# Splitting the end of each sub-layer in a two-layer decoder trunk by quarters of the residual, and moving the x transposes ahead of the last quarter and behind two k steps

## The chip, the cores and the metric

The kernel runs on 1 core of one Trainium2 chip. The time is device microseconds of one execution; before the change the median of 3 runs is 1054.25 us (1053.63 to 1054.94).

## What is computed

One sequence of 256 tokens, width 1024, goes through two layers in float32. Each layer has three sub-layers that write into x, and so six sub-layer ends, the last of which is the end of the kernel:

```python
for l in range(DEPTH):                       # DEPTH = 2
    x = x + 0.5 * swiglu(rms_norm(x, ffn1_norm[l]), ffn1_w_gate[l], ffn1_w_up[l], ffn1_w_down[l])
    h = rms_norm(x, mix_norm[l])
    proj = h @ w_in[l]                       # q, k, v, latents, rope key, two gates
    ...                                      # sliding-window attention and latent attention
    merged = sigmoid(g_a) * (o_a @ w_branch_a[l]) + sigmoid(g_b) * (o_b @ w_branch_b[l])
    x = x + merged @ w_out[l]
    x = x + 0.5 * swiglu(rms_norm(x, ffn2_norm[l]), ffn2_w_gate[l], ffn2_w_up[l], ffn2_w_down[l])
```

with `swiglu(x, g, u, d) = (silu(x @ g) * (x @ u)) @ d`, and an inner width of 2816.

## The kernel before

Every weight and every activation is split into a high part (fp32r) and a low part (the rest), and a product is three matmuls: high by high, high by low, low by high. ScalarE (ACT) writes the high part of a weight block, VectorE (DVE) the low part, and TensorE (PE) multiplies. SyncE loads a block when the slot's last low part has been written.

**FFN.** The inner width is 22 blocks of 128. `gate_up` makes gate and up of a block (8 k steps each, into PSUM banks 2b and 2b + 1, b = block parity), ACT and DVE turn them into aTh and aTl, and `down` adds the block's share of the result to the banks 4 to 7. The result has four quarters q = h * 2 + t, where h is the half of 512 columns and t the half of 128 tokens; each quarter is one bank, and takes 3 matmuls of 512 columns for a block. The loop runs `gate_up(e + 1)`, `down(e)`, and after it comes `down(21)` alone, with `stop=True` (L1450, L1485). Its quarters 0 to 2 each count up `acc_done`, the last one `d_used`.

**The end of a sub-layer.** DVE adds the quarters to x (`residual`, L943 to 955), one instruction each, and counts up `x_done`. PE transposes x to have its columns on the partitions (`columns`, L1329 to 1338): 8 columns chunks c of 128, 2 transposes each, the first four chunks when the quarters 0 and 1 of x are there, the other four when quarter 3 is. Chunk 6 and 7 reuse the banks of chunk 0 and 1, and wait until those were read (`ht_lo`). ACT multiplies a chunk by the norm's gain and writes its high part (`columns_high`, L576), DVE its low part (`columns_low`, L962). ACT squares three of the quarters for the norm (`squares`, L569, in `norm`), DVE the fourth (`last_square`, L880), then DVE adds them (`mean_square`, L887 and L889) and GpSimd (POOL) makes the inverse root (L429). ACT and DVE each work their list strictly as it is written:

```python
                def norm(n):                       # ACT
                    squares(n, 0)
                    columns_high(n)
                    squares(n, 1, (0,))
```

```python
                residual(0)                        # DVE
                columns_low(1)
                last_square(1)
                mean_square(1)
                for k in range(1, GATE1 + 1):
                    split_mix(k)
```

**What follows the end.** After the first FFN of a layer the mixer begins: PE runs the first half of gate block 0 (4 k steps of 6 matmuls of 512 columns, on chunk k), then eight `proj` blocks. Their low parts are what `split_mix(1)`, `split_mix(2)` and so on make (L833); that of gate block 0 was made within the FFN. `block_ready` makes PE wait for a block's low part. After the mixer (its last product is `w_out`, 4 blocks, 6 matmuls per quarter) and after the second FFN of layer 0 an FFN begins: `gate_up_first` takes 8 k steps of 4 matmuls, and then `spread_rs` (L1340), which multiplies the inverse root out over the partitions and waits for POOL's result. The raw sums of the gates don't depend on the root, so that nothing before needs it.

Of the kernel before, what the change touches and what calls it, by code (L numbers as in the profile page):

```python
# [59 lines left out]
X_BANK = (2, 3, 4, 6, 5, 7, 2, 3)  # L60
# [32 lines left out]
def build(nc, x_in, pos_in, cols_in, rows_in, w_ffn, w_proj, w_gate, w_uq, w_ukv, w_branch, w_out,  # L93
          masks_in, freq_in, out):
    with ExitStack() as ctx:
# [194 lines left out]
        def start_cols(i):  # L290

            c = (i % 2) * KC * P + (i // 2) * HALF
            return slice(c, c + HALF)

# [189 lines left out]
        def _(act):  # L484
# [7 lines left out]
            for l in range(DEPTH):  # L492
# [79 lines left out]
                def columns_high(n, part=range(KC)):  # L572
                    act.wait_ge(small_in.sem, small_in.per_layer * (l + 1))
                    for c in part:
                        act.wait_ge(ht_ps.sem, ht_ps.at(l, KC * n + c))
                        act.activation(hTh[:, c, :], ps[:, X_BANK[c], c // 6 * SEQ:(c // 6 + 1) * SEQ], ACT.Copy,  # L576
                                       scale=cols[:, 7 + n * KC + c:8 + n * KC + c]).then_inc(ht_hi.sem, 1)
# [245 lines left out]
        def _(dve):  # L823
# [4 lines left out]
            for l in range(DEPTH):  # L828
# [113 lines left out]
                def residual(n):  # L942

                    for h in range(2):
                        for t in range(TT):
                            q = h * TT + t
                            if q < 3:
                                dve.wait_ge(acc_done.sem, acc_done.at(l, 3 * n + q))
                            elif n == 1:
                                dve.wait_ge(gu_used.sem, gu_used.at(l, FFN2_0 - 1))  # L950
                            else:
                                dve.wait_ge(d_used.sem, d_used.at(l, FB * (n // 2 + 1) - 1))
                            part = x[:, t, h * HALF:(h + 1) * HALF]
                            factor = 0.5 if n == 1 else half_rs[:, t:t + 1]
                            dve.scalar_tensor_tensor(out=part, in0=ps[:, 4 + 2 * t + h, :], scalar=factor, in1=part,  # L955
                                                     op0=ALU.mult, op1=ALU.add).then_inc(x_done.sem, 1)

                def columns_low(n, part=range(KC)):
                    dve.wait_ge(small_in.sem, small_in.per_layer * (l + 1))
                    for c in part:  # L960
                        dve.wait_ge(ht_hi.sem, ht_hi.at(l, KC * n + c))
                        dve.scalar_tensor_tensor(out=hTl[:, c, :], in0=ps[:, X_BANK[c], c // 6 * SEQ:(c // 6 + 1) * SEQ],  # L962
# [72 lines left out]
                residual(0)  # L1035
# [9 lines left out]
                columns_low(1)  # L1045
# [238 lines left out]
                residual(1)  # L1284
                columns_low(2)
# [3 lines left out]
                residual(2)  # L1289
                if l + 1 < DEPTH:  # L1290
                    l += 1
                    columns_low(0)
# [5 lines left out]
        def _(pe):  # L1298
# [17 lines left out]
            for l in range(DEPTH):  # L1316
                def columns_start():
# [3 lines left out]
                    for c in range(KC):  # L1321
                        if c >= 6:
                            pe.wait_ge(ht_lo.sem, ht_lo.at(0, c - 6))
                        for t in range(TT):
                            ins = pe.transpose(ps[:, X_BANK[c], c // 6 * SEQ + t * P:c // 6 * SEQ + (t + 1) * P],  # L1325
                                               x[:, t, c * P:(c + 1) * P], ident[:, :])
                        ins.then_inc(ht_ps.sem, 1)

                def columns(n):  # L1329

                    for h in range(2):
                        pe.wait_ge(x_done.sem, x_done.at(l, 4 * n + (h + 1) * TT - 1 - 2 * TT))
                        for c in range(4 * h, 4 * h + 4):
                            if c >= 6:
                                pe.wait_ge(ht_lo.sem, ht_lo.at(l, KC * n + c - 6))
                            for t in range(TT):
                                ins = pe.transpose(ps[:, X_BANK[c], c // 6 * SEQ + t * P:c // 6 * SEQ + (t + 1) * P],  # L1337
                                                   x[:, t, c * P:(c + 1) * P], ident[:, :])
                            ins.then_inc(ht_ps.sem, 1)
# [34 lines left out]
                def gate_up_first(w):  # L1374
# [4 lines left out]
                    for k in range(KC):  # L1379
                        pe.wait_ge(ht_lo.sem, ht_lo.at(l, 2 * w * KC + k))  # L1380
# [69 lines left out]
                def down(w, i2, e, start=False, stop=False):  # L1450
# [4 lines left out]
                    for h in range(2):  # L1455
                        for t in range(TT):
                            ins = act_by_weight(ps[:, 4 + 2 * t + h, :], aTh[:, b, t * P:(t + 1) * P],
                                                aTl[:, b, t * P:(t + 1) * P], wh_d[b][:, h * HALF:(h + 1) * HALF],
                                                wl_d[b][:, h * HALF:(h + 1) * HALF], start, stop)
                            if stop and h * TT + t < 3:  # L1460
                                ins.then_inc(acc_done.sem, 1)
                    ins.then_inc(d_used.sem, 1)

                def ffn(w):
                    if l + w == 0:
                        columns_start()
                    else:
                        columns(2 * w)
# [12 lines left out]
                    with pe.Fori(first, FB // 2 - 1) as i:  # L1481
# [250 lines left out]
                for j in range(4):  # L1732
# [14 lines left out]
                ffn(1)  # L1747
# [63 lines left out]
```

## Time and profile before

| what | value |
|---|---|
| median of 3 runs | 1054.25 us (1053.63 to 1054.94) |
| span of the profiled execution, first to last instruction | 1051.9 us |
| what lies around the span, by the median | 2.35 us |
| granted TensorE clock over the span | 1.000 |
| busy: TensorE matmul | 1046.4 us |
| busy: TensorE weight load | 899.3 us |
| busy: VectorE | 721.1 us |
| busy: ScalarE | 593.3 us |
| DMA | 187.55 MB, mean 178 GB/s |

The profiled execution has no time of its own beside its span: the three runs shown lie 1.7 to 3.0 us above it. Busy time of TensorE's matmuls is modelled at their ends, which overlap the start of the next one, so that a short wait between two of them may not show as idle; the weight loads (PEld) show it.

### The profile page before, as it was taken

The numbers are of one execution on the slowest core, as the hardware profiler recorded it, in microseconds if no ns is written. First come the engines' busy times: TensorE is split into PE (matmuls) and PEld (weight loads), VectorE is DVE, ScalarE is ACT, GpSimd is POOL, SyncE is SP. The second block draws the span as 40 slices with busy tenths as digits, with TensorE's granted clock in tenths as the row PEclk, the third lists the DMA queues.
The fourth block names the chain that finished last, engine by engine and source line by source line (L and its number), as shares of the span: only waits on it lengthen the run. The fifth ranks groups of instructions, "written<-read, shape, count | busy, mean of one in ns | idle before, by whom it ended". The sixth has DMA issues, their size and how long they took to land.

```text
span 1051.9 us, 15566 instructions
## 1 busy us (share of the span) xinstructions
PE 1046.4 (99%) x5664; PEld 899.3 (85%) x5664; DVE 721.1 (69%) x1132; ACT 593.3 (56%) x931; POOL 66.0 (6%) x69
## 2 busy tenths in 40 slices
PE   9999999999999999999999999999999999999998
PEld 8888888898888888888888888889988888888887
DVE  6766666668786776666686666666697867666664
ACT  6555555467864655555565555555688556555552
POOL 1042000122100000000000000001211000000000
PEclk9999999999999999999999999999999999999999
DMA  7655554455335454555536445544454345554451
GB/s 261 242 203 200 202 193 144 139 180 209 126 121 200 151 209 179 182 196 203 199 136 224 180 179 182 196 166 133 157 203 158 116 165 191 208 199 180 179 182 58
DMA packets 35266, 187.55 MB, mean 178 GB/s; under 512 B 4496, under 2 KB 4640, under 8 KB 20128
## 3 DMA queue, kind: packets, MB, share of 16 engines
q1 hardware_dynamic: 34704, 186.03, 48.7%
q0 software_dynamic: 240, 0.53, 0.2%
q10 hardware_dynamic: 288, 0.54, 0.2%
q8 instruction: 20, 0.33, 0.1%
q14 instruction: 14, 0.11, 0.0%
HBM read 186.04 MB, written 1.05 MB: 178 GB/s over the span
## 4 chain that ended last, share of the span: by engine, by line
PE 99%; DVE 1%; issue 0%; ACT 0%; DVEq 0%; ACTq 0%
PE ps L1300 95%; PE ps L1337 1%; PE ps L1636 1%; PE ps L1311 1%; PE ps L1663 0%; PE ps L1699 0%; DVE x L955 0%; PE ps L1546 0%; DVE hT L962 0%; DVE S L1111 0%; PE ps L1538 0%; ACT hT L576 0%; PE ps L1325 0%; DVE w_lo L872 0%; DVE kTA L824 0%
## 5 line engine op out<-in xcount | busy, mean ns | idle before, releaser
L1300 PE MATMUL ps<-hT,w_hi 128*128 128x512 f32 x1408 | 355.4, 391 | 0.2 <-DVE hT L962 0.2
L1300 PEld LDWEIGHTS ps<-hT,w_hi 128*128 128x128 f32 x1408 | 256.3, 188 | 47.9 <-DVE hT L962 0.4
L839 DVE TENSOR_TENSOR w_lo<-w_raw,w_hi 128x2048 fp32r<-128x2048 f32 x82 | 187.9, 2292 | 73.3 <-ACT w_hi L516 73.3
L1300 PEld LDWEIGHTS ps<-hT,w_lo 128*128 128x128 f32 x1408 | 195.3, 190 | 16.0
L1300 PE MATMUL ps<-hT,w_lo 128*128 128x256 f32 x1408 | 200.0, 282 | 0.0
L1300 PE MATMUL ps<-w_hi,hT 128*128 128x512 f32 (+2 forms) x576 | 173.8, 377 | 0.0
L516 ACT ACTIVATE w_hi<-w_raw 128x2048 fp32r<-128x2048 f32 x85 | 162.3, 1910 | 18.5 <-PE ps L1300 13.2
L1300 PE MATMUL ps<-w_hi,aTh 128*128 128x512 f32 x352 | 138.2, 393 | 0.0
L1300 PE MATMUL ps<-w_lo,aTh 128*128 128x512 f32 x352 | 138.0, 392 | 0.0
L1300 PE MATMUL ps<-w_hi,aTl 128*128 128x512 f32 x352 | 137.0, 389 | 0.0
L919 DVE TENSOR_TENSOR S<-ps,S 128x256 f32<-128x256 f32 x88 | 37.3, 424 | 139.7 <-ACT S L557 139.7
L833 DVE TENSOR_TENSOR w_lo<-w_raw,w_hi 128x2048 fp32r<-128x2048 f32 (+3 forms) x54 | 101.2, 1883 | 34.6 <-ACT w_hi L504 34.6
L1300 PEld LDWEIGHTS ps<-w_hi,hT 128*128 128x128 f32 x576 | 107.4, 188 | 14.8
L504 ACT ACTIVATE w_hi<-w_raw 128x2048 fp32r<-128x2048 f32 (+3 forms) x54 | 86.0, 1593 | 55.1 <-PE ps L1300 53.0
L895 DVE TENSOR_TENSOR w_lo<-w_raw,w_hi 128x1024 fp32r<-128x1024 f32 x88 | 107.3, 1219 | 2.1 <-ACT w_hi L539 2.1
L1300 PE MATMUL ps<-w_lo,hT 128*128 128x512 f32 (+2 forms) x288 | 107.6, 374 | 0.0
L539 ACT ACTIVATE w_hi<-w_raw 128x1024 fp32r<-128x1024 f32 x88 | 93.4, 1062 | 19.1 <-PE ps L1300 19.1
L545 ACT ACTIVATE S<-ps 128x256 f32<-128x256 f32 x88 | 33.7, 383 | 121.0 <-PE ps L1300 121.0
L551 ACT ACTIVATE work<-work 128x256 f32<-128x256 f32 x88 | 36.7, 418 | 96.6 <-DVE work L908 96.6
L1300 PEld LDWEIGHTS ps<-w_hi,aTl 128*128 128x128 f32 x352 | 66.1, 188 | 14.5
L1300 PEld LDWEIGHTS ps<-w_hi,aTh 128*128 128x128 f32 x352 | 66.4, 189 | 12.1
L1300 PEld LDWEIGHTS ps<-w_lo,aTh 128*128 128x128 f32 x352 | 66.4, 189 | 10.5
(164 smaller groups left out, 961.7 us busy)
## 6 DMA issues: line engine op xcount, KB each, us to landing
w_raw<-in_w_ffn SPq DMA_DIRECT2D x85, 1024.0 KB, 5.4
w_raw<-in_w_ffn SPq DMA_DIRECT2D x92, 512.0 KB, 3.5
w_raw<-in_w_gate SPq DMA_DIRECT2D x16, 1024.0 KB, 4.9
w_raw<-in_w_proj SPq DMA_DIRECT2D x16, 592.0 KB, 4.4
w_raw<-in_w_branch SPq DMA_DIRECT2D x8, 1024.0 KB, 4.8
w_raw<-in_w_out SPq DMA_DIRECT2D x8, 1024.0 KB, 4.8
w_raw<-in_w_uq SPq DMA_DIRECT2D x4, 384.0 KB, 3.0
SG<-in_w_ffn SPq DMA_DIRECT2D x1, 1024.0 KB, 10.7
```

The source lines that it names most:

```text
L504: act.activation(mix_hi[m][:, 0:ncols], mix_raw[m][:, 0:ncols], ACT.Copy).then_inc(hi_gu.sem, 1)
L516: act.activation(wh_gu[b], raw_gu[b], ACT.Copy).then_inc(hi_gu.sem, 1)
L539: act.activation(wh_d[b], raw_d[b], ACT.Copy).then_inc(hi_d.sem, 1)
L545: act.activation(folded[:, b, 0, :], ps[:, 2 * b, SEQ:2 * SEQ], ACT.Copy).then_inc(g_low.sem, 1)
L551: act.activation(silu[:, b, :], silu[:, b, :], ACT.Silu).then_inc(silu_done.sem, 1)
L833: dve.tensor_tensor(mix_lo[m][:, 0:ncols], mix_raw[m][:, 0:ncols], mix_hi[m][:, 0:ncols].bitcast(F32), ALU.subtract).then_inc(lo_gu.sem, 1)
L839: dve.tensor_tensor(wl_gu[b], raw_gu[b], wh_gu[b].bitcast(F32), ALU.subtract).then_inc(lo_gu.sem, 1)
L895: dve.tensor_tensor(wl_d[b], raw_d[b], wh_d[b].bitcast(F32), ALU.subtract).then_inc(lo_d.sem, 1)
L919: dve.tensor_tensor(folded[:, b, 1, :], ps[:, 2 * b + 1, 0:SEQ], folded[:, b, 1, :], ALU.add)\
L1300: return pe.matmul(dst, w, m, start=start, stop=stop, skip_group_check=True)
L1311: pe.matmul(ps[:, 1, 0:P], kTA[:, 0:P], kTA[:, 0:P], start=True, stop=True, skip_group_check=True)
L1337: ins = pe.transpose(ps[:, X_BANK[c], c // 6 * SEQ + t * P:c // 6 * SEQ + (t + 1) * P], x[:, t, c * P:(c + 1) * P], ident[:, :])
```

## The change

The PE side of the last three blocks of each FFN is written out behind the loop, which is one turn shorter: `gate_up(20)`, `down(19)`, `gate_up(21)`, and `last_downs`, which replaces `down(20)` and `down(21)`. It takes quarters 0, 1, 2 of block 20, then of block 21 the high by high and high by low products of quarters 0 and 1 (waiting for `a_hi` alone), their low by high products (waiting for `a_lo`), quarter 2, then quarter 3 of block 20, then `between()`, which are the transposes of chunks 0 to 3 of the next sub-layer, and then quarter 3 of block 21. At the end of the mixer the same transposes stand ahead of quarter 3 of `w_out`'s last block. The transposes of chunks 4 to 7 stand behind the first two k steps of what follows. The bank table is another one (`X_AT`): chunks 4 and 5 share the banks of 0 and 1 (each bank holds two chunks), and wait for their low parts. On DVE the low parts of chunks 0 and 1 stand ahead of the fourth residual, and on ACT the third square stands between the high parts of chunks 3 and 4.

```diff
-X_BANK = (2, 3, 4, 6, 5, 7, 2, 3)
+X_AT_FIRST = ((2, 0), (3, 0), (4, 0), (6, 0), (5, 0), (7, 0), (2, 1), (3, 1))
+X_AT = ((2, 0), (3, 0), (4, 0), (6, 0), (2, 1), (3, 1), (5, 0), (7, 0))
...
                 def norm(n):
                     squares(n, 0)
-                    columns_high(n)
+                    columns_high(n, range(KC // 2))
                     squares(n, 1, (0,))
+                    columns_high(n, range(KC // 2, KC))
...
-                residual(0)
+                residual(0, range(3))
+                columns_low(1, range(2))
+                residual(0, (3,))
...
-                columns_low(1)
+                columns_low(1, range(2, KC))
                 last_square(1)
                 mean_square(1)
...
+                def transposed(layer, n, h):
+
+                    for c in range(4 * h, 4 * h + 4):
+                        if c in (4, 5):
+                            pe.wait_ge(ht_lo.sem, ht_lo.at(layer, KC * n + c - 4))
+                        dst = x_place(layer, n, c)
+                        for t in range(TT):
+                            ins = pe.transpose(dst[:, t * P:(t + 1) * P], x[:, t, c * P:(c + 1) * P], ident[:, :])
+                        ins.then_inc(ht_ps.sem, 1)
...
+                def columns(layer, n, h):
+
+                    pe.wait_ge(x_done.sem, x_done.at(layer, 4 * n + (h + 1) * TT - 1 - 2 * TT))
+                    transposed(layer, n, h)
...
                     for k in range(KC):
+                        if k == 2:
+                            columns(l, 2 * w, 1)
                         pe.wait_ge(ht_lo.sem, ht_lo.at(l, 2 * w * KC + k))
...
+                def last_downs(w, between):
...
+                    pe.wait_ge(lo_d.sem, lo_d.at(l, w * FB + FB - 2))
+                    pe.wait_ge(a_lo.sem, a_lo.at(l, w * FB + FB - 2))
+                    for q in range(3):
+                        quarter(FB - 2, q, range(3))
+                    pe.wait_ge(lo_d.sem, lo_d.at(l, w * FB + FB - 1))
+                    pe.wait_ge(a_hi.sem, a_hi.at(l, w * FB + FB - 1))
+                    for q in range(2):
+                        quarter(FB - 1, q, range(2))
+                    pe.wait_ge(a_lo.sem, a_lo.at(l, w * FB + FB - 1))
+                    for q in range(2):
+                        quarter(FB - 1, q, (2,)).then_inc(acc_done.sem, 1)
+                    quarter(FB - 1, 2, range(3)).then_inc(acc_done.sem, 1)
+                    quarter(FB - 2, 3, range(3)).then_inc(d_used.sem, 1)
+                    between()
+                    quarter(FB - 1, 3, range(3)).then_inc(d_used.sem, 1)
...
-                    with pe.Fori(first, FB // 2 - 1) as i:
+                    with pe.Fori(first, FB // 2 - 2) as i:
                         for b in range(2):
                             gate_up(w, i * 2, 2 + b)
                             down(w, i * 2, 1 + b)
-                    down(w, 0, FB - 1, stop=True)
+                    gate_up(w, 0, FB - 2)
+                    down(w, 0, FB - 3)
+                    gate_up(w, 0, FB - 1)
+                    last_downs(w, between)
...
-                ffn(0)
-
-                columns(1)
+                ffn(0, lambda: columns(l, 1, 0))
+
                 hi, lo = block_ready(at_block("gate", 0))
                 for k in range(KC // 2):
+                    if k == 2:
+                        columns(l, 1, 1)
...
                         for t in range(TT):
+                            if j == 3 and h * TT + t == 3:
+                                columns(l, 2, 0)
...
-                ffn(1)
+                ffn(1, lambda: columns(l + 1, 0, 0) if l + 1 < DEPTH else None)
```

Where the instructions stand. At the end of an FFN ahead of the mixer, on PE, the start of the last block was

```order
L1481 COMPARE_AND_BRANCH
L1300 MATMUL ps<-w_hi,aTh 128x512 [waits a_lo,lo_d]
L1300 MATMUL ps<-w_lo,aTh 128x512
L1300 MATMUL ps<-w_hi,aTl 128x512
L1300 MATMUL ps<-w_hi,aTh 128x512
```

and is in the change, with three matmuls of block 20 fewer in front of it,

```order
L1313 MATMUL ps<-w_hi,aTl 128x512
L1313 MATMUL ps<-w_hi,aTh 128x512 [waits a_hi,lo_d]
L1313 MATMUL ps<-w_lo,aTh 128x512
L1313 MATMUL ps<-w_hi,aTh 128x512
L1313 MATMUL ps<-w_lo,aTh 128x512
L1313 MATMUL ps<-w_hi,aTl 128x512 [waits a_lo]
```

So the first matmul of block 21 comes three matmuls earlier, and waits for aTh and no longer for aTl.

From the last matmuls of the FFN to the first of the gate block (hT is the transposed x) PE had

```order
L1300 MATMUL ps<-w_hi,aTl 128x512
L1337 MATMUL ps<-ident,x 128x128 [waits x_done]
L1337 MATMUL ps<-ident,x 128x128 x7
L1337 MATMUL ps<-ident,x 128x128 [waits x_done]
L1337 MATMUL ps<-ident,x 128x128 x3
L1337 MATMUL ps<-ident,x 128x128 [waits ht_lo]
L1337 MATMUL ps<-ident,x 128x128
L1337 MATMUL ps<-ident,x 128x128 [waits ht_lo]
L1337 MATMUL ps<-ident,x 128x128
L1300 MATMUL ps<-w_hi,hT 128x512 [waits ht_lo,lo_gu]
```

and has in the change, here and after two k steps of the gate block,

```order
L1313 MATMUL ps<-w_hi,aTl 128x512
L1337 MATMUL ps<-ident,x 128x128 [waits x_done]
L1337 MATMUL ps<-ident,x 128x128 x7
L1313 MATMUL ps<-w_hi,aTh 128x512
L1313 MATMUL ps<-w_lo,aTh 128x512
L1313 MATMUL ps<-w_hi,aTl 128x512
L1313 MATMUL ps<-w_hi,hT 128x512 [waits ht_lo,lo_gu]
...
L1337 MATMUL ps<-ident,x 128x128 [waits ht_lo,x_done]
L1337 MATMUL ps<-ident,x 128x128
L1337 MATMUL ps<-ident,x 128x128 [waits ht_lo]
L1337 MATMUL ps<-ident,x 128x128 x5
```

Eight of the sixteen transposes moved three matmuls ahead, the other eight twelve matmuls of the gate block back.

On DVE, at the same place, stood

```order
L955 SCALAR_TENSOR_TENSOR x<-ps,half_rs,x 128x512 [waits acc_done] x2
L955 SCALAR_TENSOR_TENSOR x<-ps,half_rs,x 128x512 [waits d_used]
L962 SCALAR_TENSOR_TENSOR hT<-ps,cols,hT 128x256 [waits ht_hi,small_in]
L962 SCALAR_TENSOR_TENSOR hT<-ps,cols,hT 128x256 [waits ht_hi] x7
L880 SCALAR_TENSOR_TENSOR sq,ss<-x 128x512 [waits x_done]
L887 TENSOR_TENSOR rs_step<-ss 128x2 [waits ss_done]
L889 TENSOR_SCALAR rs_step<-rs_step 128x2 [waits ms_sum]
L833 TENSOR_TENSOR w_lo<-w_raw,w_hi 128x1184 [waits hi_gu] x8
```

and stands now

```order
L961 SCALAR_TENSOR_TENSOR x<-ps,half_rs,x 128x512 [waits acc_done] x2
L968 SCALAR_TENSOR_TENSOR hT<-ps,cols,hT 128x256 [waits ht_hi,small_in]
L968 SCALAR_TENSOR_TENSOR hT<-ps,cols,hT 128x256 [waits ht_hi]
L961 SCALAR_TENSOR_TENSOR x<-ps,half_rs,x 128x512 [waits d_used]
L968 SCALAR_TENSOR_TENSOR hT<-ps,cols,hT 128x256 [waits ht_hi,small_in]
L968 SCALAR_TENSOR_TENSOR hT<-ps,cols,hT 128x256 [waits ht_hi] x5
L887 SCALAR_TENSOR_TENSOR sq,ss<-x 128x512 [waits x_done]
L894 TENSOR_TENSOR rs_step<-ss 128x2 [waits ss_done]
L896 TENSOR_SCALAR rs_step<-rs_step 128x2 [waits ms_sum]
L840 TENSOR_TENSOR w_lo<-w_raw,w_hi 128x1184 [waits hi_gu] x8
```

The fourth residual moved behind two low parts; the squares, the mean and the low parts of the `proj` blocks stand behind the low part of chunk 7 as before.

## Rows read from the trace of the kernel before

**Rows 1.** The page, part 1: busy time of each engine.

```profile
PE 1046.4 (99%) x5664; PEld 899.3 (85%) x5664; DVE 721.1 (69%) x1132; ACT 593.3 (56%) x931; POOL 66.0 (6%) x69
```

**Rows 2.** Line L1337, the transposes: what TensorE idled for before them (us, times).

```profile
  DVE hT L962: 1.9, 10
  DVE x L955: 0.6, 3
```

**Rows 3.** Timeline, first FFN end to gate block: start us, length, engine, line, operation, count.

```profile
187.04 0.19 PEld L1300 LDWEIGHTS ps<-w_hi,aTh 128*128 128x128 f32 x1
187.15 0.40 PE L1300 MATMUL ps<-w_hi,aTh 128*128 128x512 f32 x1
...
188.76 0.42 ACT L563 ACTIVATE aTh<-work 128x256 fp32r<-128x256 f32 x1 [1.02 <-DVE work L927]
...
190.35 0.39 PE L1300 MATMUL ps<-w_hi,aTl 128*128 128x512 f32 x1
...
190.86 2.73 DVE L955 SCALAR_TENSOR_TENSOR x<-ps,half_rs,x 128x512 f32<-128x512 f32 x4 [1.23 <-PE ps L1300]
...
192.30 0.63 ACT L569 ACTIVATE SG<-x 128x512 f32<-128x512 f32 x1
192.39 0.39 PE L1300 MATMUL ps<-w_hi,aTl 128*128 128x512 f32 x1
...
192.62 2.42 PE L1337 MATMUL ps<-ident,x 128*128 128x128 f32 x16
...
193.10 3.03 ACT L576 ACTIVATE hT<-ps,cols 128x256 fp32r<-128x256 f32 x8
193.64 0.42 PEld L1337 LDWEIGHTS ps<-ident,x 128*128 128x128 f32 x4 [0.22 <-DVE x L955]
193.68 3.23 DVE L962 SCALAR_TENSOR_TENSOR hT<-ps,cols,hT 128x256 fp32r<-128x256 f32 x8
194.22 0.20 PEld L1337 LDWEIGHTS ps<-ident,x 128*128 128x128 f32 x2 [0.16 <-DVE hT L962]
...
195.12 0.39 PE L1300 MATMUL ps<-w_lo,hT 128*128 128x512 f32 x1
```

**Rows 4.** The same timeline, later: the norm's end, the proj blocks' low parts, a load.

```profile
196.82 0.68 DVE L880 SCALAR_TENSOR_TENSOR sq<-x 128x512 f32<-128x512 f32 x1
...
197.82 2.69 DVE L833 TENSOR_TENSOR w_lo<-w_raw,w_hi 128x1184 fp32r<-128x1184 f32 x2
...
199.23 0.33 SPq L321 DMA_DIRECT2D w_raw<-in_w_proj  x1
```

**Rows 5.** Timeline of PE: the gate block's end and the first proj matmuls.

```profile
200.13 0.56 PE L1300 MATMUL ps<-w_hi,hT 128*128 128x512 f32 x2
```

**Rows 6.** Timeline: twelve transposes between two gate matmuls inside the mixer.

```profile
263.57 0.39 PE L1300 MATMUL ps<-w_hi,hT 128*128 128x512 f32 x1
...
265.35 0.40 PE L1300 MATMUL ps<-w_lo,hT 128*128 128x512 f32 x1
```

**Rows 7.** Timeline: start of the second FFN, to the spreading of the root.

```profile
345.77 0.63 PE L1300 MATMUL ps<-hT,w_hi 128*128 128x512 f32 x2
...
346.31 0.68 DVE L880 SCALAR_TENSOR_TENSOR sq<-x 128x512 f32<-128x512 f32 x1
...
347.47 1.60 POOL L429 TENSOR_TENSOR rs<-rs_step,minus_half 128x2 f32<-128x2 f32 x1 [75.41 <-DVE rs_step L889]
...
349.83 0.53 PEld L1300 LDWEIGHTS ps<-ident,rs 128*128 128x128 f32 x4
```

**Rows 8.** Timeline: the kernel's end.

```profile
1046.59 2.75 DVE L955 SCALAR_TENSOR_TENSOR x<-ps,half_rs,x 128x512 f32<-128x512 f32 x4 [1.24 <-PE ps L1300]
...
1048.16 0.39 PE L1300 MATMUL ps<-w_hi,aTl 128*128 128x512 f32 x1
```

**Rows 9.** Windows: us, busy time by engine, granted clock (PEclk), DMA share, GB/s.

```profile
192.00:195.00 3.00, 3.00 (x21) 2.27 (x20) 2.91 (x7) 2.93 (x10) 0.00 (x0) 1.00 0.00 0
...
1048.00:1052.00 4.00, 0.55 (x3) 0.12 (x1) 1.34 (x3) 0.00 (x0) 0.00 (x0) 0.93 0.70 262
```

More of the change, by code:

```diff
@@ L293, in start_cols, with x_place @@
             return slice(c, c + HALF)
+        def x_place(layer, n, c):
+            bank, half = (X_AT_FIRST if layer + n == 0 else X_AT)[c]
+            return ps[:, bank, half * SEQ:(half + 1) * SEQ]
         block = ctx.enter_context(nc.Block())
@@ L940, in prod_low @@
                        .then_inc(a_lo.sem, 1)
[L942 to L956, printed above, removed]
@@ L958, in columns_low, with residual @@
-                def columns_low(n, part=range(KC)):
-                    dve.wait_ge(small_in.sem, small_in.per_layer * (l + 1))
+                def residual(n, quarters=range(2 * TT)):
+                    for q in quarters:
+                        h, t = divmod(q, TT)
+                        if q < 3:
+                            dve.wait_ge(acc_done.sem, acc_done.at(l, 3 * n + q))
+                        elif n == 1:
+                            dve.wait_ge(gu_used.sem, gu_used.at(l, FFN2_0 - 1))
+                        else:
+                            dve.wait_ge(d_used.sem, d_used.at(l, FB * (n // 2 + 1) - 1))
+                        part = x[:, t, h * HALF:(h + 1) * HALF]
+                        factor = 0.5 if n == 1 else half_rs[:, t:t + 1]
+                        dve.scalar_tensor_tensor(out=part, in0=ps[:, 4 + 2 * t + h, :], scalar=factor, in1=part,
+                                                 op0=ALU.mult, op1=ALU.add).then_inc(x_done.sem, 1)
@@ L1448, in gate_up_third, with down @@
                         ins.then_inc(sig.sem, 1)
-                def down(w, i2, e, start=False, stop=False):
+                def down(w, i2, e, start=False):
                     b = e % 2
@@ L1458, in down, with quarter, ffn @@
                                                 aTl[:, b, t * P:(t + 1) * P], wh_d[b][:, h * HALF:(h + 1) * HALF],
[L1459 to L1461 removed]
+                                                wl_d[b][:, h * HALF:(h + 1) * HALF], start, False)
                     ins.then_inc(d_used.sem, 1)
[L1464 removed]
+                def last_downs(w, between):
+                    def quarter(e, q, passes):
+                        b = e % 2
+                        h, t = divmod(q, TT)
+                        hi, lo = (a[:, b, t * P:(t + 1) * P] for a in (aTh, aTl))
+                        part = slice(h * HALF, (h + 1) * HALF)
+                        for p in passes:
+                            ins = mm(ps[:, 4 + 2 * t + h, :], (hi, hi, lo)[p], (wh_d, wl_d, wh_d)[p][b][:, part], False,
+                                     e == FB - 1 and p == 2)
+                        return ins
+                    pe.wait_ge(lo_d.sem, lo_d.at(l, w * FB + FB - 2))
[13 more added lines that the diff above has]
+                    quarter(FB - 1, 3, range(3)).then_inc(d_used.sem, 1)
+                def ffn(w, between):
                     if l + w == 0:
                         columns_start()
[L1467 to L1468 removed]
                     gate_up_first(w)
```

35 lines of the change are left out of this document (16 added, 19 removed).

## The prediction

> **What bounds the kernel now.** I read the page's busy times first, then what the transposes waited for, then the timeline around each end of a sub-layer, and last the windows. TensorE's matmuls are busy 1046.4 us of a span of 1051.9 [rows 1], so nothing else can be the bound for long, and a change that removes no matmul can only win the time in which TensorE stands between two matmuls. By that row there is next to none. The weight loads tell more: before the transposes of line L1337 they stood 1.9 us for low parts of x (10 times) and 0.6 us for a residual (3 times), 2.5 us in all [rows 2]. Perfetto Trace Analysis in the Trainium skill (Identifying the Most-Contended Engine) says that matmul busy time hides headroom and weight loads don't; by the matmul row the sum of what can be won would be 0, by the loads 2.5. The trace agrees with the page: the window 192 to 195 shows the matmuls 3.00 of 3.00 busy over three such waits [rows 9].
>
> How much one end costs: a 512 column matmul takes 0.228 us of the stream (187.15 to 192.39 is 23 of them) [rows 3]. From the last FFN matmul (192.39) to the second gate matmul (195.12) are 2.73 us, less 2 x 0.228 is 2.27 for 16 transposes [rows 3]. Twelve transposes without a wait cost 265.35 - 263.57 - 2 x 0.228 = 1.32, or 0.11 each, and no more for going in and out [rows 6]. So 16 need 1.76, and **0.51 us is waiting**. The other two FFN ends look the same, the two ends of w_out's product come to 0.53. All five: 2.6 us, or 0.25%. That is all that the change can win there, and about 0.2% is what a measurement of this kernel can tell from no change.
>
> **The change part by part.** Number of matmuls and transposes, loads and DMAs stay as they are; the shorter loop removes one branch per FFN, which I cost at nothing (a turn is 99% matmuls either way). What counts is who now waits. I set times on the first FFN end (FFN to mixer), where block 20's down starts at 187.15.
>
> *The earlier block 21.* It comes 9 matmuls after 187.15, at 189.20, its load a matmul before that (188.98). It needs aTh, which is done at 188.76 + 0.42 = 189.18 [rows 3]. A load starts 0.05 after the release (residual's end 193.59, load 193.64), and the matmul 0.11 after its load (187.04, 187.15): 189.34. New wait 0.15 (0 if the queue hides it, 0.3 if the releases take longer), at all four FFNs.
>
> *Transposes ahead of quarter 3.* Quarter 0 is done with the 14th matmul instead of the 15th. DVE starts 0.51 after such a matmul starts (190.35, 190.86) [rows 3], so at 187.15 + 13 x 0.228 + 0.15 + 0.51 = 190.77. ACT's square of quarter 1 starts at 192.30, so that quarter 1 was there by 192.25, 1.39 after DVE's start; now at 190.77 + 1.39 = 192.16, and with load and matmul the first transpose can go at 192.32. The stream would have it at 187.15 + 21 x 0.228 + 0.15 = 192.09: wait 0.23. Before, the transposes stood behind three more matmuls, and this was hidden.
>
> *The first k step.* ACT squares quarter 1 from 192.21 and takes up chunk 0 after 0.80 (192.30, 193.10), at 193.01; DVE's low part starts 0.58 later, 193.59 (193.10, 193.68), and frees PE's load 0.54 later, 194.13 (193.68, 194.22); matmul at 194.24 [rows 3]. The stream is there at 192.32 + 0.88 (8 transposes) + 3 x 0.228 = 193.89: wait 0.35. The three new waits, 0.15 + 0.23 + 0.35 = **0.73, replace 0.51**.
>
> *The other eight transposes, ahead of the mixer.* They start after two k steps of six matmuls, at T = 194.24 + 12 x 0.228 = 196.98; quarter 3's residual and chunks 0 and 1 are long done. Nothing is late for them. What is late stands behind them. ACT takes chunk 4 at T + 0.48 (192.62, 193.10), DVE at T + 1.06; a chunk takes 0.39 (193.68 to 196.82 for 8), so the last square starts at T + 1.06 + 4 x 0.39 = T + 2.63, and the low part of the first proj block 1.00 later (196.82, 197.82). The load that waits for that low part goes out 1.41 after its start (199.23) [rows 3, 4]: **ready at T + 5.04**. PE needs this low part after 8 transposes and 12 more matmuls, at T + 0.88 + 2.74 = T + 3.62; with 0.11 from load to matmul it starts at T + 5.15. **New wait 1.53 us.** Before, it was ready at 199.23 and wanted by the second matmul of [rows 5], at 200.13 + 0.228 = 200.36 (its load at 200.25), 1.0 to spare. Nothing else covers it: PE's next instruction is the proj matmul, and DVE can't do the block earlier, for it is behind the chunks in its list. ACT's high part of the second proj block is later by about 2 us too, but a block is 18 matmuls long, over 3 us. The load behind 199.23 goes out 2.8 later; it is for the slot's next block, three blocks on. I cost both at nothing; if they were not covered, up to 1 us each.
>
> This end in sum: +0.73 - 0.51 + 1.53 = +1.75. It is there in both layers: **+3.5**. Bounds of the 1.53: DVE and ACT times are those of the same instructions, so 1.3 to 1.8.
>
> *The ends of w_out's product, ahead of the second FFN.* Here quarters are six matmuls apart (1.37), so neither the residual nor the low part is waited for, and the 0.53 goes away. The eight late transposes start at T' = 345.77 (third k step) - 0.53 - 0.88 = 344.36 [rows 7]. The last square starts at T' + 2.63 = 346.99, 0.68 later than before, and POOL has the root 2.76 after (346.31, 347.47 + 1.60), at 349.75; PE's load for the spreading can go at 349.80, where it went at 349.83 [rows 7]. The stream would be there at 349.83 - 0.53 = 349.30. **The 0.53 turns into a wait of 0.50 for the root.** Two ends: -0.06.
>
> *FFN to FFN, between the layers.* The same three waits, and the root: 0.73 - 0.51 + 0.50 = +0.72.
>
> *The kernel's end.* The four residuals ran 2.75 from 1046.59, at a pitch of 0.67 ((2.73 - 1.39) / 2), the last from 1048.60, about when the last matmul (1048.16) lets it go at the soonest, 1048.16 + 0.51 = 1048.67 [rows 8]. With the new wait of 0.15 ahead of that matmul it starts at 1048.82: +0.2. The early quarters win nothing at the end.
>
> **Sum:** 3.5 - 0.06 + 0.72 + 0.2 = +4.4 us. The profiled execution's span of 1051.9 becomes 1056.3; with the 2.35 between span and median, **1058.7**.
>
> **Rivals.**
> *All waits go (faster).* One mechanism: the five ends lose their 0.51 to 0.53 and no wait takes their place, 1054.25 - 2.6 = 1051.7. It decides at T + 3.62: if the proj block's low part (and the root) were there by then. For it: that part was ready 1.0 us before it was wanted. Against: the last square was at 196.82 when the chunks were done by 195, and now PE itself hands the chunks over 2 us later. 0.04.
> *The mixer's wait is hidden, the small ones are not.* If DVE's chain of five low parts, square and mean ran 1.5 us shorter than rows say, or PE had other work: 4.4 - 3.1 = +1.3, 1055.6, within 0.2%. 0.09.
> *The clock falls at the new wait.* The granted clock is 1.00 over every window with waits, and falls only where TensorE has finished (0.93 over 1048 to 1052) [rows 9], which is 2.4 down to 1.2 GHz for a part of it. If it fell at the two mixer waits for one proj block each (18 matmuls, some 3.2 us longer at half speed): 1058.7 + 6.5 = 1065. Against: in no window before the end did it move. TensorE: Matmul & The Clock Gate in the Trainium skill (Part 4: PE-mode transpose) says that transposes don't count as work for the clock; by it the 16 transposes of a present end, waits among them, should have been the place to see a fall, and the trace shows 1.00 over 192 to 195, so it doesn't bear it out here. 0.03.
> *The forecast*, +4.4: 0.84.
>
> **How the numbers follow.** Bounds of the forecast: aTh wait 0 to 0.3 at four places, the mixer's wait 1.3 to 1.8 at two, the root's 0.3 to 0.7 at three, the load and ACT behind +1: about -1.6 to +1.9, so 1057.1 to 1060.6. The lower end goes to 1056.2 to take in part of the second rival. Slower by over 0.2% (above 1056.4): 0.87; within: 0.09; faster: 0.04.
>
> **What would show it.** In the changed profile: a wait of PE (or its loads) for the low part w_lo of the first proj block, 1.5 us, twice, and waits of 0.5 for POOL's root three times; waits before the transposes ahead of quarter 3 near 0.25 at FFN ends, those before the first matmul of hT 0.35 at FFN ends and none behind w_out; no wait for low parts at chunks 4 to 7. From the last FFN matmul but three to the first proj matmul each layer takes 1.75 us longer. I am wrong if the first proj block starts without a wait, or if the FFN ahead of the root runs through.

## The result, and where the time went

The changed kernel takes 1057.37 us (median of 6 runs, 1056.94 to 1057.52), the kernel before beside it 1053.94 us (6 runs, 1053.08 to 1054.94): a ratio of 1.0033, with a 95% interval of 1.0024 to 1.0043. It is slower, by 3.4 us, where +4.4 on the span and 1058.7 in all were forecast. The span went from 1051.9 to 1055.6 us, +3.7.

The page's span and busy times, to be held against [rows 1]:

```profile
span 1055.6 us, 15558 instructions
## 1 busy us (share of the span) xinstructions
PE 1047.0 (99%) x5664; PEld 898.9 (85%) x5664; DVE 721.0 (68%) x1132; ACT 593.2 (56%) x931; POOL 68.0 (6%) x69
```

TensorE's busy time is the same to 0.6 us, while the span grew by 3.7: what was added is nearly all standing time. What TensorE's matmuls waited for (line, releaser and its line: us in all, times, longest):

```profile
PE ps L1313 <- DVE w_lo L840: 2.6, 2, 1.3
...
PE ps L1313 <- POOL rs L435: 0.5, 3, 0.2
```

and its weight loads:

```profile
PEld ps L1337 <- DVE x L961: 1.2, 3, 0.4
PEld ps L1313 <- POOL rs L435: 1.1, 3, 0.4
```

The ten waits of the transposes for low parts of x [rows 2] have gone. In their place stand two waits for w_lo of the mixer's first proj block and three for POOL's root, and the three for a residual have doubled. Seven more stand in the loads' rows under `issue`, the profile's word where it names no releaser: 0.33 us ahead of the last block's first product (aTh) at all four FFNs, where 0.11 stood before, and 0.41 ahead of the first matmul of hT at three FFN ends. Here is the first FFN end, which answers to [rows 3 to 5] (timeline: start us, length, engine, line, operation, count, and in brackets the idle time before):

```profile
189.29 0.19 PEld L1313 LDWEIGHTS ps<-w_hi,aTh 128*128 128x128 f32 x1 [0.33 <-issue]
...
190.84 2.07 DVE L961 SCALAR_TENSOR_TENSOR x<-ps,half_rs,x 128x512 f32<-128x512 f32 x3 [1.20 <-PE ps L1313]
...
192.29 0.86 PEld L1337 LDWEIGHTS ps<-ident,x 128*128 128x128 f32 x8 [0.39 <-DVE x L961]
192.30 1.09 PE L1337 MATMUL ps<-ident,x 128*128 128x128 f32 x8
...
194.07 0.19 PEld L1313 LDWEIGHTS ps<-w_hi,hT 128*128 128x128 f32 x1 [0.41 <-issue]
194.10 0.47 PE L1313 MATMUL ps<-w_hi,hT 128*128 128x512 f32 x1
...
196.93 1.04 PE L1337 MATMUL ps<-ident,x 128*128 128x128 f32 x8
197.41 1.57 ACT L582 ACTIVATE hT<-ps,cols 128x256 fp32r<-128x256 f32 x4 [2.34 <-PE ps L1337]
...
197.91 1.66 DVE L968 SCALAR_TENSOR_TENSOR hT<-ps,cols,hT 128x256 fp32r<-128x256 f32 x4 [2.13 <-ACT hT L582]
...
199.49 0.68 DVE L887 SCALAR_TENSOR_TENSOR sq<-x 128x512 f32<-128x512 f32 x1
...
200.49 3.99 DVE L840 TENSOR_TENSOR w_lo<-w_raw,w_hi 128x1184 fp32r<-128x1184 f32 x3
...
201.90 2.93 SPq L327 DMA_DIRECT2D w_raw<-in_w_proj  x3
201.99 0.19 PEld L1313 LDWEIGHTS ps<-w_hi,hT 128*128 128x128 f32 x1 [1.72 <-issue]
202.02 0.41 PE L1313 MATMUL ps<-w_hi,hT 128*128 128x384 f32 x1 [1.32 <-DVE w_lo L840]
```

Read it from the bottom. The proj matmul starts at 202.02 after 1.32 idle, on VectorE's w_lo (200.49, the first of three in that group). That stands behind the square (199.49), the square behind four low parts (197.91), these behind ScalarE's four (197.41), and these behind the eight late transposes (196.93). Between 195.8 and 197.9 VectorE did nothing: the row of L968 shows 2.13 idle before it. It had time for w_lo there, but not the turn.

A ledger tells where the 3.8 us arose. Each line is the start of the same matmul in both traces, and what the difference grew by since the line above:

| marker (TensorE) | before | after | difference | grew by | forecast |
|---|---|---|---|---|---|
| first down matmul | 26.61 | 26.61 | 0 | | |
| first low-part matmul of proj, layer 0 | 200.53 | 202.27 | +1.74 | +1.74 | +1.75 |
| first down of the second FFN | 355.99 | 357.64 | +1.65 | -0.09 | -0.03 |
| last loop turn of that FFN begins | 522.3 | 523.8 | +1.50 | -0.15 | 0 |
| first down, layer 1 | 541.73 | 543.77 | +2.04 | +0.54 | +0.72 |
| proj, layer 1 | 721.28 | 725.01 | +3.73 | +1.69 | +1.75 |
| first down of the last FFN | 876.74 | 880.36 | +3.62 | -0.11 | -0.03 |
| last matmul | 1048.16 | 1051.94 | +3.78 | +0.15 | +0.2 |

The -0.15 inside the second FFN is not the change's: its loop turns take 8.31 us, but now and then one takes 0.05 to 0.4 longer (before: 8.38 and 8.45, after: one of 8.37), in other turns, or in none, in the traces below. In the two longest (8.62 and 8.72) TensorE's loads wait 0.4 and 0.5 for VectorE's aTl; what makes it late there, no run asks.

### The profile page after: what moved, and what is told of

Same layout as the page of the kernel before. It is cut to its first block, busy times and chain, and to the rows that moved or that the text cites. A ratio compares the mean times of both kernels' runs of the same rounds, so it can differ in the third digit from the quotient of the medians.

```text
span 1055.6 us, 15558 instructions
## 1 busy us (share of the span) xinstructions
PE 1047.0 (99%) x5664; PEld 898.9 (85%) x5664; DVE 721.0 (68%) x1132; ACT 593.2 (56%) x931; POOL 68.0 (6%) x69
## 4 chain that ended last, share of the span: by engine, by line
PE 97%; DVE 2%; POOL 0%; ACT 0%; issue 0%; ACTq 0%; DVEq 0%; POOLq 0%
PE ps L1313 94%; PE ps L1683 1%; DVE hT L968 1%; PE ps L1337 1%; PE ps L1324 1%; PE ps L1710 0%; POOL rs L435 0%; PE ps L1746 0%; DVE sq L887 0%; ACT hT L582 0%; DVE w_lo L840 0%; PE ps L1593 0%; DVE S L1119 0%; PE ps L1585 0%; DVE rs_step L896 0%
```

## The experiments

Beside each median stands that of the kernel before, run in between on the same chip, and the ledger's last line: the time from the first down matmul to the last matmul, less the 1021.55 us of the kernel before. The ledger leaves out the start, which varies by up to 0.6 us with the first loads.

| kernel | median us | before | ratio (95%) | ledger |
|---|---|---|---|---|
| the change | 1057.37 | 1053.94 | 1.0033 (1.0024 to 1.0043) | +3.78 |
| + w_lo first | 1054.21 | 1053.47 | 1.0007 (0.9998 to 1.0016) | +0.56 |
| + root first | 1056.03 | 1053.47 | 1.0024 (1.0015 to 1.0033) | +2.68 |
| + both first | 1052.94 | 1053.47 | 0.9995 (0.9986 to 1.0004) | -0.19 |
| late transposes behind 1 k step | 1054.23 | 1053.58 | 1.0006 (0.9997 to 1.0016) | +1.11 |
| behind 3 k steps | 1063.04 | 1053.58 | 1.0091 (1.0075 to 1.0106) | +9.99 |
| behind 3 k steps, w_lo first | 1055.14 | 1053.59 | 1.0016 (1.0007 to 1.0025) | +1.71 |
| both first, whole downs | 1053.58 | 1053.58 | 0.9999 (0.9990 to 1.0008) | -0.14 |
| w_out's ends alone, root late | 1053.13 | 1053.58 | 0.9994 (0.9985 to 1.0003) | -0.44 |
| w_out's ends alone, root first | 1051.99 | 1053.47 | 0.9986 (0.9977 to 0.9995) | -1.26 |
| the same, paired banks | 1051.11 | 1053.59 | 0.9978 (0.9969 to 0.9987) | -2.22 |

**w_lo first.** One line of VectorE's list is moved:

```diff
+                split_mix(1)
                 columns_low(1, range(2, KC))
                 last_square(1)
                 mean_square(1)
-                for k in range(1, GATE1 + 1):
+                for k in range(2, GATE1 + 1):
                     split_mix(k)
```

> The changed kernel with one operation moved in VectorE's list: the low part of the mixer's first proj block is made right after the fourth residual, ahead of the low parts of x's chunks 2 to 7, the last square and the mean. Theory (the time is VectorE's list behind the late transposes): the wait of 1.3 us of the second proj matmul for w_lo goes at both mixer ends and with it the delay of 1.5 each; 2.9 to 3.1 us less than the changed kernel, about 1054.4. Rival (the time comes from the quartered downs and their waits for aTh, the residual and the first k step, or from the longer program): unchanged, 1057.4, though the wait has gone. A third way: the low part, 1.3 us long, now makes chunk 2 late for its k step, and the gain is half, about 1055.9.

Measured: 3.2 us less in the ledger, 0.0026 less in the ratio. Both waits are gone. The timeline at the same place:

```profile
194.81 1.38 DVE L840 TENSOR_TENSOR w_lo<-w_raw,w_hi 128x1184 fp32r<-128x1184 f32 x1
...
200.18 0.56 PE L1314 MATMUL ps<-w_hi,hT 128*128 128x512 f32 x2
...
200.58 0.34 PE L1314 MATMUL ps<-w_lo,hT 128*128 128x384 f32 x1
```

The low part now lies in the 2.13 us that VectorE idled, and TensorE goes from the gate's last matmul into proj without a gap. Each mixer end gives back 1.59 (from +1.74 to +0.15) and 1.57 (from +1.69 to +0.12). Five sixths of the change's whole cost (3.16 of 3.78) are the place of one 1.4 us operation in one engine's list, and the quartered downs with their waits are not it.

**Root first.** Last square and mean go ahead of the low parts of chunks 4 to 7, at the three ends that are followed by an FFN:

```diff
-                columns_low(2, range(2, KC))
+                columns_low(2, range(2, KC // 2))
                 last_square(2)
                 mean_square(2)
+                columns_low(2, range(KC // 2, KC))
...
-                    columns_low(0, range(2, KC), l)
+                    columns_low(0, range(2, KC // 2), l)
                     last_square(0)
                     mean_square(0)
+                    columns_low(0, range(KC // 2, KC), l)
```

> The changed kernel with VectorE's last square and mean of squares ahead of the low parts of chunks 4 to 7, at the three ends that are followed by an FFN. Theory: the spreading of the root waits for nothing any more, 0.3 us less at three places, 0.9 in all, about 1056.5; the mixer's waits for w_lo stay at 1.3. Rival (these waits cost nothing, since the loads run ahead of the matmuls): unchanged, 1057.4.

Measured: 0.0009 less in the ratio, as the theory has it, with the waits for POOL gone from the list. In the ledger w_out's ends go from -0.09 and -0.11 to -0.50 and -0.52, and the FFN to FFN end from +0.54 to +0.09 (last loop turn to first down: 19.94 to 19.49; 19.40 in the kernel before). So the late root costs 0.41, 0.41 and 0.45. The expectation had said 0.3, from the matmul's rows; the loads' row (0.4 the longest, 1.1 in three) is what the removal measured. Two slow loop turns (8.40 and 8.41) took back 0.2 of it in the one trace.

**Both.** The two edits together.

> Both moves at once, w_lo of the first proj block and last square and mean ahead of the late low parts. Theory: the two add, since they lie at different ends: 3.8 to 4.0 us less than the changed kernel, about 1053.5, which is 0.5 below the kernel before: what is left is the three small waits at the FFN ends (0.75 against 0.51 before, three times) and the kernel's end (0.15) against the 0.53 won at the two w_out ends. Rival: 1057.4 if the time lies in the quartered downs.

Measured: the two add up (ledger -0.19, which is 3.97 less than the change), and the kernel is level with the one before. What it shows is the change without its two new waits: w_out's ends give 0.52 each, which is all that was there, and the three FFN ends cost +0.21, +0.08 and +0.15 more than the ones they replace.

**The late transposes behind one k step, and behind three.** Only the number in `if k == 2:` ahead of the mixer's late transposes is another.

> The changed kernel with the mixer's late transposes behind one k step instead of two; VectorE's order as in the changed kernel. Theory (VectorE takes up the late low parts when TensorE hands them over, and w_lo stands behind them): the whole chain starts 6 matmuls (1.37 us) earlier, so the wait for w_lo shrinks from 1.5 to 0.1 to 0.2 at each mixer end; 2.7 less than the changed kernel. Rival (w_lo is late for a reason of its own, its weights or ScalarE's rounding): no change.

Measured: 2.67 less in the ledger, and no wait for w_lo left; proj of layer 0 stands at +0.38 instead of +1.74, 1.36 less against the 1.37 that six matmuls take. The chain from hand-over to w_lo is rigid, and starts with the transposes.

> The changed kernel with the mixer's late transposes behind three k steps instead of two. Theory: the chain starts 1.37 us later and the wait for w_lo grows by as much at each mixer end, to 2.9; 2.7 more than the changed kernel. Rival: no change, or less than 1 us, if the chunks or w_lo are not what is late.

Measured: 6.2 more in the ledger, where the theory said 2.7. The wait itself is as forecast, and something else comes behind it:

```profile
202.88 0.45 PE L1313 MATMUL ps<-w_hi,hT 128*128 128x384 f32 x1 [2.67 <-DVE w_lo L840]
...
203.44 0.84 PE L1313 MATMUL ps<-w_hi,hT 128*128 128x384 f32 x2
...
204.08 0.52 PE L1313 MATMUL ps<-w_lo,hT 128*128 128x384 f32 x1
204.09 0.65 PEld L1313 LDWEIGHTS ps<-w_hi,hT 128*128 128x128 f32 x2
```

Windows over the same stretch, first of this kernel, then of the change (us; busy time of PE, PEld, DVE, ACT, POOL; granted clock; DMA share, GB/s):

```profile
200.00:202.80 2.80, 0.20 (x1) 0.00 (x0) 2.73 (x8) 1.99 (x2) 1.21 (x1) 1.00 0.00 0
202.80:204.00 1.20, 1.12 (x4) 1.15 (x5) 1.20 (x2) 0.00 (x0) 1.11 (x2) 0.63 0.27 36
204.00:206.00 2.00, 2.00 (x7) 1.95 (x7) 1.33 (x2) 0.00 (x0) 1.41 (x2) 0.50 0.93 302
206.00:206.50 0.50, 0.50 (x3) 0.50 (x3) 0.00 (x0) 0.00 (x0) 0.00 (x0) 0.50 0.72 152
206.50:208.00 1.50, 1.50 (x10) 1.50 (x9) 0.00 (x0) 0.01 (x1) 0.00 (x0) 0.99 0.88 314
```

```profile
200.00:202.80 2.80, 1.48 (x9) 1.04 (x8) 2.73 (x6) 1.26 (x2) 1.98 (x2) 1.00 0.00 0
202.80:204.00 1.20, 1.20 (x8) 1.20 (x8) 1.20 (x2) 0.00 (x0) 1.10 (x2) 1.00 0.83 174
204.00:206.00 2.00, 2.00 (x13) 1.99 (x12) 0.48 (x1) 0.41 (x1) 0.65 (x1) 1.00 0.92 311
```

After a wait of 2.67 us the granted clock is 0.50, that is 1.2 GHz instead of 2.4, until 206.5; the count of matmuls in 204 to 206 is 7, where the change has 13 there. From proj's first low part to the root's spreading this kernel takes 150.79 us (203.13 to 353.92), the change 149.23: **1.56 us for the clock**, beside 1.36 for the longer wait. Twice both is 5.8 of the 6.2, and most of the rest are two slow loop turns of this trace (8.72 and 8.42). At the other mixer end the wait is 2.68 and the clock 0.50 over 729 to 732. The median is of four runs, 1061.96, 1063.02, 1063.06 and 1064.58 us, at a mean clock of 0.998, 0.996, 0.997 and 0.995: the fastest has the highest clock and the slowest the lowest. So how often or how long the clock is down seems to differ from run to run, but only the run of 1063.06 us has a trace. Behind the change's wait of 1.32 us the clock stays at 1.00. So the prediction's third rival is a real mechanism, one k step further on than where it was looked for, and at half the price that the prediction gave it (3.25 an end).

Is it the late transposes or the wait that brings the clock down? The same kernel with w_lo first:

> The changed kernel with the mixer's late transposes behind three k steps, but the low part of the first proj block made ahead of the low parts of chunks 2 to 7. Theory: without the wait of 2.7 us for w_lo the granted clock does not fall either, and the time is that of the version with two k steps and w_lo first (1.0007 of the kernel before), within 0.3 us. Rival (the clock falls, or the delay stays, because the transposes stand later): 2 us or more above that version.

Measured: the granted clock is 1.00 over 198 to 206, and 8.3 of the 10 us in the ledger are gone, so it is the wait, and not the place of the transposes. The other half of the expectation failed: the kernel is 1.15 above the version with two k steps, not within 0.3. Its timeline shows why:

```profile
198.66 1.66 DVE L968 SCALAR_TENSOR_TENSOR hT<-ps,cols,hT 128x256 fp32r<-128x256 f32 x4 [2.17 <-ACT hT L582]
...
200.38 0.44 PE L1314 MATMUL ps<-w_hi,hT 128*128 128x384 f32 x1 [0.30 <-DVE hT L968]
```

With only six matmuls between the late transposes and proj, the low part of the last chunk (done at 200.32) is itself late for proj's first matmul; that is 0.57 and 0.60 at the two ends. I had looked at w_lo alone and not at the next term of the same list.

**Whole downs.** With both moves kept, the last two down blocks are whole again and in the old order, the first eight transposes behind them (the new function, a loop of `act_by_weight` over the quarters, is not shown).

> The kernel with both moves in VectorE's list (w_lo first, last square and mean first), but the last two down blocks of each FFN whole and in the old order again, with the first eight transposes behind them; the other eight stay behind two k steps. Theory: with whole blocks the waits for aTh (0.15) and for x (0.23) go, and that of the first k step grows from 0.35 to 0.8, since it is the same chain from the residual by transpose, ScalarE and VectorE; so 0.1 more at each of three FFN ends and 0.2 less at the kernel's end, the same as the kernel with both moves within 0.3. Rival (the quarters are what wins at the FFN ends): 0.5 or more at each of three ends, 1.5 slower than it.

Measured: ledger -0.14 against -0.19, medians 1053.58 and 1052.94 against 1053.58 and 1053.47 for the kernel before: no difference that the medians can tell. The ledger shows a small one once the slow loop turns are taken out, of which the trace of both first has two (8.62 and 8.43, 0.43 us in all) and this one none. The whole downs lose 0.23, 0.26 and 0.20 at the three FFN ends and win 0.22 at the kernel's end, 0.5 us in sum: twice the 0.1 an end that was expected, and about half of the rival's 0.5. The first hT matmul of this version starts at 194.32 and its transposes at 192.64; less 0.88 for eight of them that is a wait of 0.80, as expected, in place of the three small ones. By quarters or whole, the FFN end runs at the pace of one chain: residual, transpose, ScalarE's copy, VectorE's low part. The quarters mostly choose where along it TensorE stands, and win some 0.2 of it.

**The change at w_out's ends alone.** If the FFN ends gain nothing, they can stay as they were. The next two kernels have `columns` in one piece ahead of the mixer and of the FFN between the layers, with the old places in PSUM, and the split with two k steps only ahead of the second FFN; one has the root first there, the other late. The last blocks of an FFN stay written out behind the shorter loop in both.

> The kernel before, with the change at the two ends of w_out's product alone (half of the transposes ahead of the last quarter, the rest behind two k steps) and there the last square and mean ahead of the late low parts; the FFN ends are as before, downs whole and transposes in one piece. Theory: each w_out end loses its 0.53 us and gets no new wait: 1.06 less than the kernel before, about 1052.9. Rival (transposes between matmuls of another product cost something, or the wait moves on into the FFN): no change, 1053.9.

> The kernel that has the change at w_out's two ends alone, without the early square and mean: VectorE does them behind the low part of chunk 7, as in the changed kernel. Theory: each of the two ends gives 0.1 instead of 0.5, as the root is late again: 0.2 less than the kernel before, 0.85 more than the version with them early. Rival: the same as that version, 1.0 or more less than before.

Measured: 1.26 less than before in the ledger with the root first, of which w_out's ends are 0.53 and 0.50 (and 0.2 the slow loop turns of the trace of before), and 0.44 less with the root late, of which they are 0.07 and 0.08. The first FFN with its end, up to proj, takes the same as before in both (0.00 and +0.01), so the written-out blocks cost nothing. By the medians the first is 1.5 faster than before, the first kernel here with an interval below 1 (0.9977 to 0.9995). With the square early, POOL's root not only starts sooner, it is also shorter. The root in the version with the root late, then in the one with the root first:

```profile
347.96 2.35 DVE L859 TENSOR_TENSOR w_lo<-w_raw,w_hi 128x1024 fp32r<-128x1024 f32 x2
...
348.13 1.60 POOL L435 TENSOR_TENSOR rs<-rs_step,minus_half 128x2 f32<-128x2 f32 x1 [76.05 <-DVE rs_step L899]
```

```profile
345.08 1.66 DVE L971 SCALAR_TENSOR_TENSOR hT<-ps,cols,hT 128x256 fp32r<-128x256 f32 x4
...
345.25 0.70 POOL L435 TENSOR_TENSOR rs<-rs_step,minus_half 128x2 f32<-128x2 f32 x1 [73.69 <-DVE rs_step L899]
```

**Paired banks.** What is left of the 0.51 at the FFN ends was, by [rows 2], mostly chunks 6 and 7, which are written into the banks of chunks 0 and 1 and wait for their low parts. On top of the last version they go beside chunks 4 and 5:

```diff
+X_AT_PAIRS = ((2, 0), (3, 0), (4, 0), (6, 0), (5, 0), (7, 0), (5, 1), (7, 1))
...
                         act.wait_ge(ht_ps.sem, ht_ps.at(l, KC * n + c))
+                        if n < 2 and l + n > 0 and c >= 6:
+                            act.wait_ge(ht_lo.sem, ht_lo.at(l, KC * n + c - 2))
...
-                    for c in range(4 * h, 4 * h + 4):
+                    for c in (4, 6, 5, 7) if pairs else range(4 * h, 4 * h + 4):
...
```

> The version with the change at w_out's ends alone, and at the FFN ends chunks 6 and 7 of the transposes put into the second halves of the banks of chunks 4 and 5 (order 4, 6, 5, 7) instead of those of chunks 0 and 1, so that they no longer wait for the low parts of chunks 0 and 1; ScalarE's rounding of chunks 6 and 7 waits for the low parts of 4 and 5 instead. Theory: of the 0.51 us at each FFN end some 0.15 waits for the residual and stays, and about 0.36 is this wait and goes, three times: 1.1 less than the version without it, 2.1 to 2.5 less than the kernel before. Rival (the wait moves to the first k step, which needs the same low part of chunk 0): the same as the version without it, 1.0 to 1.5 less than before.

Measured: 0.96 less in the ledger than without it, 0.31 to 0.37 at each of the three ends, and 1051.11 us:

```profile
192.24 2.11 PE L1340 MATMUL ps<-ident,x 128*128 128x128 f32 x16
...
193.25 0.86 PEld L1340 LDWEIGHTS ps<-ident,x 128*128 128x128 f32 x8 [0.22 <-DVE x L967]
...
194.10 0.48 PE L1315 MATMUL ps<-w_hi,hT 128*128 128x512 f32 x1
```

The sixteen transposes run through, but for one load's 0.22 for the last residual. This version is 2.5 us faster than the kernel before and 5.8 faster than the change (0.0055 by the ratios): it beats both. Whether the paired banks without any split would do as well at w_out's ends, no run asks.

## Why the prediction was right, and where it was off

The forecast of slower held, and by its mechanism. Point by point:

*What bounds the kernel, and what could be won.* 2.6 us of standing at five ends was the most. The w_out ends gave 0.52 and 0.50 with the root first, against 0.53; the paired banks took 0.96 out of three times 0.51. Both together are 2.0 of the 2.6.

*The small waits at an FFN end, 0.15, 0.23 and 0.35.* All three are there, in the loads' rows as 0.33, 0.39 and 0.41. In the stream they are less: the first matmul of hT starts at 194.10, where 194.24 was reckoned.

*The eight late transposes ahead of the mixer, +1.53 each.* Right. Chunk 4 was taken up by ScalarE 0.48 after the transposes (196.93, 197.41) and by VectorE 0.98 after (197.91; 1.06 was reckoned), the square started 2.56 after them (2.63), w_lo 3.56 (3.63). Taking the wait away gave 1.59 and 1.57. With the transposes six matmuls earlier or later, proj of layer 0 moved by 1.36 both ways.

*The first FFN end in sum, +1.75.* +1.74 and +1.69. That it comes out to 0.01 in layer 0 is in part luck: the wait for w_lo was 0.06 more than reckoned, the small waits 0.07 less. The three small new waits less the old 0.51, +0.22 in the sum, are +0.15 and +0.12 with w_lo first, and +0.21 and +0.15 with both first.

*The ends of w_out's product, -0.03 each.* -0.09 and -0.11. "The 0.53 turns into a wait of 0.50 for the root" is what happened; the root's wait is 0.41. It was sized from the root's time in the trace of before plus the 0.68 by which the square comes later, and each of these was good to about 0.1. The root's own time, though, hangs on what VectorE does beside it (last section): this was reckoned as fixed, and it held because w_lo stood beside it in both kernels.

*FFN to FFN, +0.72.* This is the term that was mis-sized the most: +0.54. The root is 0.45 of it for 0.50, and the small waits +0.09 for +0.22. That the small waits are less here than ahead of the mixer is measured (19.49 and 19.47 against 19.40); why, I did not follow up.

*The kernel's end, +0.2.* The last matmul is 0.15 later.

*What was costed at nothing.* The load behind w_lo, ScalarE's high parts and the shorter loop: behind proj's first block, up to w_out's end, the loads' rows of the change show the same waits as before, and the versions with w_out's ends alone show none for the loop.

*The range.* Its upper end, +1.9, doesn't follow from the bounds listed: the waits alone come to 4 x 0.15 + 2 x 0.27 + 3 x 0.2 = 1.7, and with +1 for the load and ScalarE to 2.7. The time came out below the forecast, so that this end was not tried.

*From span to time.* The terms measured add up to 3.92, and the slow loop turns of the trace of before take 0.15 off, so the span's part of the miss is 0.7 us (4.4 for 3.7). The other 0.6 is the 2.35 that I added between span and median: it was the distance of one execution's span to the median of other executions. In every later kernel the profiled execution's own time lies 1.8 us above its span (the change: 1057.36 and 1055.6). With 1.8 the same sum gives 1058.1.

*The rivals.* All waits go: the ten waits went, as it says, and others took their place. The mixer's wait hidden: it stood in the open at both ends. The clock: not in the change, where it is 1.00 through both waits, but real at a wait twice as long. The page's rule that transposes don't count as work (Trainium skill, TensorE: Matmul & The Clock Gate, Part 4) is neither borne out nor refuted here. The clock is 1.00 over 16 transposes in a row in the version with paired banks (192 to 195) as it was in [rows 9], but these take 2.1 us, and that lies between the wait of 1.32 behind which the clock stayed and the one of 2.67 behind which it fell. The prediction took [rows 9] for more than it is.

## What to carry to other kernels

When work is handed to an engine later, list what stands behind it in that engine's own order, and follow each of those to its reader: the cost of this change was a 1.4 us operation that had been 1.0 us early and was queued behind work that now came 2 us later, while the engine idled. An in-order engine that idles ahead of late work is a free place; fill it with whatever was next. Splitting a tail to overlap it won all of the wait where the pieces are six matmuls apart (w_out, 0.5 us with the root early), and lost 0.1 to 0.2 where they are three apart (the FFN's end), which is too short to cover the chain between them; so measure the pieces one end at a time.

## What the runs showed of the hardware

**POOL's root beside VectorE.** The 128x2 root on POOL takes 0.70 to 0.72 us in all thirteen places where VectorE meanwhile makes low parts of x from one input in PSUM and one in SBUF (three each in the versions with the root first, with both first and with whole downs, two each in those with w_out's ends alone and the root first, without and with paired banks), and 1.55 to 1.73 us in the other 59 of the twelve traces, where a w_lo, with two inputs in SBUF, is under way on VectorE when it starts. Those 59 all end 0.55 to 0.59 us after the end of that VectorE instruction, be it 1.22 or 1.38 us long (with the root late above: the first of the two w_lo ends at 347.96 + 1.22 = 349.18, the root at 348.13 + 1.60 = 349.73). They read as if POOL stood until that instruction was through. That is 0.9 us for the company it keeps, twice the root's whole wait. The Trainium skill names such a contention (GPSIMD Engine Reference, Specifications: the SBUF interface is shared with VectorE instructions that have two SBUF inputs); the rows agree, and give its size. The profile's spans on POOL are rough, but these fall into two groups with nothing between. No run changes the company alone, with the root's place kept.

**The clock after a wait.** TensorE, at work before, stood 2.67 us and then ran at 0.50 of its clock, 1.2 GHz, up to 206.5: matmuls of 384 columns came 0.32 us apart (204.08 - 203.44, two of them) where they are 0.18 apart else. That cost 1.56 us. So it went at both mixer ends of that trace. After a wait of 1.32 us it ran on at 1.00.

**Which row tells the price of a short wait.** For the root, the matmuls' row says 0.17 a time, the loads' row 0.38, and taking it away gave 0.41 to 0.45. A matmul's modelled end (0.39 after its start, where the next one starts after 0.23) covers part of the gap behind it. For w_lo the matmul's row says 1.32 and the load's 1.72, put down to `issue` and not to w_lo, where the removal gave 1.58. So the loads' row was the better guide for the root, and the true price of w_lo lies between the two.
